# Scores of the latent attention: three rounded products in place of one plain fp32 product

## The reference

```
c      = rmsnorm(c_kv, kv_norm)                         # 512 tokens x 128
q_lat  = einsum('bthd,hdc->bthc', qh, w_uk) * 64**-0.5  # 6 heads, 512 queries x 128
logits = einsum('bqhc,bqkc->bqhk', q_lat, c_sel)        # over the selected tokens
prob   = softmax(where(valid, logits, -inf))
o_lat  = einsum('bqhk,bqkc->bqhc', prob, c_sel)
out    = einsum('bqhc,hcd->bqhd', o_lat, w_uv)
```

## Time and profile before

| | |
|---|---|
| median of three runs | 3670.35 us |
| profiled execution | 3665.43 us |
| its span, first to last instruction | 3663.6 us |
| mean granted TensorE clock | 0.991 of full speed |
| TensorE busy, weight loads | 3566.1 us, 3092.2 us |
| VectorE, ScalarE, GpSimd busy | 2024.6, 1430.8, 176.9 us |
| DMA | 303.22 MB, mean 83 GB/s |

### The profile page before, as it was taken

The page is one execution under the profiler, slowest core; times in us unless marked ns, Lnnn a source line. Parts: engine busy times, 40 slices in busy tenths (PEclk is TensorE's granted clock), DMA queues, the critical chain, the costliest instruction groups (busy, mean ns, idle before and its releaser), DMA issues. The chain is left out here.

```text
span 3663.6 us, 61588 instructions
## 1 busy us (share of the span) xinstructions
PE 3566.1 (97%) x26295; PEld 3092.2 (84%) x26295; DVE 2024.6 (55%) x3372; ACT 1430.8 (39%) x2289; POOL 176.9 (5%) x220
## 2 busy tenths in 40 slices
PE   9999999899999999999999999999999999999998
PEld 8999999788899998888877678888888877678887
DVE  7667663544476646544478564444444468664443
ACT  6844332554453323322244353223232244353222
POOL 0000000111000001000004100000000004100000
PEclk9999999999999999999999999999999999999999
DMA  3232333122223332333320023333333320023332
GB/s 137 81 99 81 93 88 92 65 77 76 68 71 93 91 90 80 98 97 95 115 75 3 24 81 98 98 91 105 95 96 94 111 86 3 24 70 98 98 93 80
DMA packets 87873, 303.22 MB, mean 83 GB/s; under 512 B 9632, under 2 KB 11808, under 8 KB 87344
## 3 DMA queue, kind: packets, MB, share of 16 engines
q1 hardware_dynamic: 87600, 299.28, 26.6%
HBM read 297.11 MB, written 2.13 MB: 82 GB/s over the span
## 5 line engine op out<-in xcount | busy, mean ns | idle before, releaser
L698 DVE TENSOR_TENSOR two_w_lo<-one_raw,two_w_hi 128x1024 fp32r<-128x1024 f32 (+1 forms) x333 | 399.3, 1200 | 749.9 <-ACT two_w_hi L690 747.7
L713 PE MATMUL psum<-two_x_hi,two_w_hi 128*128 128x512 f32 x1768 | 695.1, 393 | 1.1 <-DVE two_rows L1592 0.9
L713 PE MATMUL psum<-two_x_hi,two_w_lo 128*128 128x512 f32 x1768 | 688.4, 389 | 0.0
L713 PE MATMUL psum<-two_x_lo,two_w_hi 128*128 128x512 f32 x1768 | 688.0, 389 | 0.0
L690 ACT CAST two_w_hi<-one_raw 128x1024 fp32r<-128x1024 f32 (+1 forms) x333 | 340.9, 1025 | 803.0 <-PE psum L713 803.0
L713 PEld LDWEIGHTS psum<-two_x_hi,two_w_hi 128*128 128x128 f32 x1768 | 331.8, 188 | 91.3 <-issue 22.1
L2404 PE MATMUL psum<-one_x_hi,one_w_hi 128*128 128x264 f32 (+1 forms) x1376 | 391.6, 285 | 7.9 <-DVE one_x_lo L798 7.3
L713 PEld LDWEIGHTS psum<-two_x_hi,two_w_lo 128*128 128x128 f32 x1768 | 331.9, 188 | 69.7
L713 PEld LDWEIGHTS psum<-two_x_lo,two_w_hi 128*128 128x128 f32 x1768 | 332.0, 188 | 69.5 <-issue 1.4
L2404 PE MATMUL psum<-one_x_lo,one_w_hi 128*128 128x264 f32 (+1 forms) x1376 | 389.3, 283 | 0.0
L2404 PE MATMUL psum<-one_x_hi,one_w_lo 128*128 128x264 f32 (+1 forms) x1376 | 388.7, 282 | 0.0
(11 more groups left out here) (563 smaller groups left out, 6733.9 us busy)
## 6 DMA issues: line engine op xcount, KB each, us to landing
one_raw<-in_swi_in SPq DMA_DIRECT2D x172, 512.0 KB, 3.6
one_raw<-in_ffn_in SPq DMA_DIRECT2D x88, 512.0 KB, 3.8
one_raw<-in_swi_out SPq DMA_DIRECT2D x64, 448.0 KB, 3.3
one_raw<-in_mix_in SPq DMA_DIRECT2D x54, 512.0 KB, 3.6
one_raw<-in_attn_w SPq DMA_DIRECT2D x32, 512.0 KB, 3.9
one_raw<-in_swi_out SPq DMA_DIRECT2D x32, 512.0 KB, 3.6
one_raw<-in_ffn_out SPq DMA_DIRECT2D x32, 448.0 KB, 3.3
one_raw<-in_lru_w SPq DMA_DIRECT2D x24, 512.0 KB, 5.2
```

The lines of the kernel that those rows point to most:

```text
L698: self.nc.vector.tensor_tensor(lo, self.m.raw[:, u % self.RAW, 0:self.cols(u)], hi.bitcast(FP32), ALU.subtract).then_inc(self.s["w_lo"], 1)
L713: last = self.nc.tensor.matmul(self.m.ps[:, bank, :], a[:, w], b[:, k0 + k, :], start=(start and k == 0 and q == 0), stop=(stop and k == n ...
```

## The change

Queries and tokens are split. ScalarE's eviction of a latent query now writes the rounded part (`q_hi`), and VectorE subtracts that from the scaled product in PSUM (`query_rest`, `q_lo`). ScalarE copies the normalised tokens to a rounded tile (`c_hi`), VectorE subtracts again (`c_lo`). Each score is lo x hi, hi x hi and hi x lo in one PSUM group. A bank of the latent queries is now free when VectorE's subtraction is done, so TensorE waits for `q_rest` where it waited for `q_out`. On VectorE, the eviction of score 3 goes behind the subtractions 2 and 3, and L3642 behind all of them.

```diff
+    m.late_q_hi = place("late_q_hi", [P, 6, SEQ], hidden, FP32R)
+    m.late_q_lo = [place("late_q_lo", [P, 5, SEQ], hidden + 60 * KB + 8 * 532 * 4, FP32R),
+                   place("late_q_lo5", [P, 1, SEQ], hidden + 60 * KB + 6 * 532 * 4, FP32R)]
+    m.late_c = Split(place("late_c_hi", [P, SEQ], base + KT * T1 * 4 + (19 * SEQ + 384) * 4, FP32R),
+                     place("late_c_lo", [P, SEQ], hidden + 52 * KB + 2 * SEQ * 4, FP32R))
...
 tensor, latent_query(h):
                     pe.wait_ge(s["q_out"], h - 1)
+                    pe.wait_ge(s["q_rest"], h - 1)
 tensor, score(i):
                     if b == 0:
-                        pe.wait_ge(s["c_ready"], 1)
-                        pe.wait_ge(s["q_out"], h + 1)
-                    nc.tensor.matmul(m.ps[:, bank(i), 0:(b + 1) * QB], e.qlat[:, h, b * QB:(b + 1) * QB],
-                                     c_lat[:, 0:(b + 1) * QB], start=True, stop=True).then_inc(s["scored"], 1)
+                        pe.wait_ge(s["c_rest"], 1)
+                        pe.wait_ge(s["q_rest"], h + 1)
+                    out, queries, n = m.ps[:, bank(i), 0:(b + 1) * QB], slice(b * QB, (b + 1) * QB), (b + 1) * QB
+                    nc.tensor.matmul(out, e.q_lo[h][:, queries], e.c_hi[:, 0:n], start=True, stop=False)
+                    nc.tensor.matmul(out, e.q_hi[h][:, queries], e.c_hi[:, 0:n], start=False, stop=False)
+                    nc.tensor.matmul(out, e.q_hi[h][:, queries], e.c_lo[:, 0:n], start=False, stop=True).then_inc(
+                        s["scored"], 1)
 tensor, ahead of the spreads (L3368):
-            pe.wait_ge(s["q_out"], H)
+            pe.wait_ge(s["q_rest"], H)
 scalar:
-                nc.scalar.mul(e.qlat[:, h, :], m.ps[:, 2 + h % 2, :], SCALE).then_inc(s["q_out"], 1)
+                nc.scalar.mul(e.q_hi[h], m.ps[:, 2 + h % 2, :], SCALE).then_inc(s["q_out"], 1)
...
             for h in range(2, H):
                 latent_query(h)
+            act.wait_ge(s["c_ready"], 1)
+            nc.scalar.copy(e.c_hi, c_lat).then_inc(s["c_rounded"], 1)
 vector:
+            def query_rest(h):
+                dve.wait_ge(s["q_out"], h + 1)
+                nc.vector.scalar_tensor_tensor(e.q_lo[h], m.ps[:, 2 + h % 2, :], SCALE, e.q_hi[h].bitcast(FP32), ALU.mult,
+                                               ALU.subtract).then_inc(s["q_rest"], 1)
...
             evict(2)
+            query_rest(0)
+            query_rest(1)
...
             nc.vector.reciprocal(e.factor, e.factor).then_inc(s["f_factor"], 1)
+            query_rest(2)
+            query_rest(3)
             evict(3)
+            query_rest(4)
+            query_rest(5)
+            dve.wait_ge(s["c_rounded"], 1)
+            nc.vector.tensor_tensor(e.c_lo, c_lat, e.c_hi.bitcast(FP32), ALU.subtract).then_inc(s["c_rest"], 1)
             dve.wait_ge(s["ahead_hi"], 1)
```

More of the change, by code:

```diff
@@ L3297, in __init__ @@
         slot = lambda t, i: t[:, i * SEQ:(i + 1) * SEQ]
-        self.qlat = m.low[:, 0:6 * SEQ].rearrange("p (n t) -> p n t", t=SEQ)
+        self.q_hi = [m.late_q_hi[:, h, :] for h in range(6)]
+        self.q_lo = [*[m.late_q_lo[0][:, h, :] for h in range(5)], m.late_q_lo[1][:, 0, :]]
+        self.c_hi, self.c_lo = m.late_c.hi[:, :], m.late_c.lo[:, :]
         self.olat = m.high[:, 0:6 * SEQ].rearrange("p (n t) -> p n t", t=SEQ)
@@ L3348, in mixers_end_stage @@
                "f_factor", "spread", "normed", "c_squared", "c_gained", "c_sums", "c_root", "c_factor", "c_spread", "c_ready",
-               "c_psum", "tok_ready", "q_psum", "q_out", "scored", "evicted",
+               "c_psum", "tok_ready", "q_psum", "q_out", "q_rest", "c_rounded", "c_rest", "scored", "evicted",
                "shift_ready", "exp_done", "own", "gained", "boosted", "prob_ready", "probT_psum", "probT_ready", "out_psum", "out_ready",
```

## The result

The changed kernel takes 3679.02 us (median of 20 runs, 3670.06 to 3688.63); the kernel before takes 3668.03 beside it (20 runs, 3662.91 to 3674.91). The ratio is 1.0029, with an interval of 1.0021 to 1.0038: about 11 us slower, where the prediction had 0.4 us less and a range that ended at 3678. Times follow the mean granted clock of each run: the two shortest, 3670.06 and 3670.94, had 0.989, the longest, 3688.63, had 0.982. The profiled execution took 3683.35 us at 0.985.

What follows compares the result with a forecast made beforehand. TensorE, 97% busy, was taken as the bound in the last attention steps; other steps wait for VectorE. Head +0.35 and +0.5, loop 2 x -0.6: -0.4 us, so 3665.0 profiled, 3670.0 on the median; range 3662 to 3678.

Steps and rivals of the forecast that it cites:

- the loop's 128-column term: Six 128-column scores per layer: three hidden by waits, three count, one of them twice at half clock; +0.4 us.
- if the clock shares stay: Condition on the two stretches' forecast lengths, about 88.6 and 87.1 us: time at 1.2 GHz unchanged.
- The clock: Rival: one 1.2 GHz stretch more or less in each layer, plus or minus 3.4 us, 3666.6 or 3673.4; chance 0.16.
- The new waits make the head thinner: Clock rival's slower way: TensorE may fall to 1.2 GHz in the head once more, 3673.4; half of chance 0.16.
- denser scores may do the reverse: Clock rival's faster way: one 1.2 GHz stretch less in each layer, 3666.6; half of chance 0.16.
- The rival of dear narrow products: Rounded 128-column products cost 0.222 us, the pace of plain ones, in each layer's first six steps; +4.5, 3674.5; chance 0.11.
- 256 columns: Loop's six 256-column scores per layer: no long wait for probabilities, so all six count; -0.4 us.
- 384 columns: Loop's six 384-column scores per layer: five hidden by waits or ScalarE-set steps, one counts; -0.1 us.
- 512 columns: Loop's six 512-column scores per layer: three hidden by waits or VectorE's work, three count; -0.5 us.
- The head: Stage before the loop: query 4 newly waits for VectorE's subtraction; +0.35 us in the first layer, +0.5 in the second.
- two signs of this: In the head: L3425 0.35 and 0.5 us later; late L3646 following the 1.21 us subtraction without gap means VectorE bounds.
- Theory A of the expectations: From the experiments: at 128 columns weight loads set the pace, operands move half the time; low traffic keeps clock down.

Runs made afterwards that it cites:

- the second experiment: Changed kernel with three rounded products per score (hi x hi three times), but head and waits as before, no remainders or subtractions; 3678.76 us, 1.0025 to the kernel before.
- the first two experiments: From the changed kernel: all scores plain with its head kept, 3671.80 us, 1.0004; three rounded products with the head of before, 3678.76 us, 1.0025.
- the padded and filled kernel: Changed kernel with 128-column scores made 256 wide and five unused 512-column rounded products at the stage's end; 3663.04 us, 0.9988 to the kernel before.

## Why the prediction was wrong

**The step that failed** is the clock in the loop's 128-column term. That one score "falls into a half-clock stretch" carried the stretch of before over unchanged, and the whole sum stood on "if the clock shares stay". Of that term's +0.4 us a layer the narrow steps measured +3.9 and +4.1 (20.96 and 21.07 against 17.05 and 16.99); the 256-column steps of after add 2.8 and 0.8 to that, 13.71 and 11.63 us in place of the 10.87 that they take at full clock in the second experiment.

The clock stood among the rivals, with sign open, and the price of one stretch was about right: the second experiment's narrow steps, at clock 0.90 and 0.75, spend a fifth and a half of their 17.26 and 20.46 us at the lower level, 3.5 and 10.2 us, so 3.2 us go with 6.8, 1.6 for each 3.4, where the rival had 1.7. Its count was wrong, one stretch more in each layer, where the loop has four more and three more. So was its reason. "The new waits make the head thinner" is refuted as the cause of the loss by the first two experiments, and "denser scores may do the reverse" had it backwards for the narrow ones. I took a fuller TensorE for a safer clock, and did not ask what the clock would do under narrow rounded products, of which before has no row.

**What held, at equal clock.** The rounded steps of the second experiment's first layer against those of before:

- 128 columns: +0.2 (17.26 against 17.05), predicted +0.4. The rival of dear narrow products falls: starts are 0.11 us apart.
- 256 columns: 10.87 against 11.18, -0.3, predicted -0.4.
- 384 columns: 13.11 against 13.43, -0.3, predicted -0.1: more of them count than I had taken to stand ahead of a wait.
- 512 columns: 11.03 + 10.66 to the last eviction against 11.33 + 10.75, -0.4, predicted -0.5. The last score-to-score period is 2.02 us (2138.69 to 2140.71 in after), where it was 2.19 and 2.0 was forecast.

Together -0.8 us a layer, where the sum had -0.6. That gain is real, and the clock takes back several times as much. Rounding nothing but the wide scores shows no gain, 1.0004; half a microsecond a layer is below what runs can tell.

**The head.** From the stage's first matmul to the first latent score, with 3.4 us at 1.2 GHz inside, it takes 22.64 us before (second layer) and 22.83 after (first); with 6.8 us inside, 24.27 (first) and 24.66 (second): +0.2 and +0.4, where +0.35 and +0.5 were forecast. The forecast named two signs of this, and the timeline of after shows them:

```profile
2072.87 1.09 ACT L3531 ACTIVATE two_late_q_hi<-psum 128x512 fp32r<-128x512 f32 x2 [2.31 <-PE psum L3386]
...
2076.32 0.86 PE L3436 MATMUL psum<-two_ring,two_misc 128*64 128x384 f32 x2
...
2078.86 1.22 DVE L3668 TENSOR_TENSOR two_ahead_lo<-two_ahead_raw,two_ahead_hi 128x1024 fp32r<-128x1024 f32 x1
2079.99 2.06 DVE L3672 TENSOR_TENSOR two_ring<-two_ring,psum 128x512 f32<-128x512 f32 x3
```

Counted from the eviction of queries 2 and 3, L3436 (L3425 before) starts after 3.45 us, against 2.63 in the earlier trace rows; in the second layer after 3.08 (3194.03 to 3197.11) against 2.43 in the earlier trace rows. That is 0.8 and 0.65 later, where 0.35 and 0.5 were forecast, but the clocks differ: 2.2 of these 3.45 us lie at 1.2 GHz against 0.4 of 2.63, in the second layer 0.6 against none. At 1.6 us for each 3.4 that can make up to 0.8 and 0.3 of the delay. Part of it is given back before the first score. And the three scalings (L3672, L3646 before) follow the 1.22 us subtraction without a gap: VectorE is the head's bound there, as the other sign had it. It costs a few tenths of a microsecond.

**The account.** First stage: 13.7 us more at 1.2 GHz in the loop and 3.4 less in the head, at 1.6 for each 3.4 us, give +4.8; with -0.8 and +0.2 that is +4.2, and +4.3 was measured. Second: 10.3 us more in the loop and 3.4 more in the head give +6.4; with -0.8 and +0.4 that is +6.0, and +5.9 was measured. The head's stretches vary in all kernels alike; what belongs to the change is the loop's 13.7 and 10.3 us, 11 us together. The median lost the same, though its runs need not split it so.

**What stays open:** what it is in the narrow rounded products that the clock answers to. With two, three or four of them a score the clock stays down, with the same three at 256 columns it doesn't; further the runs don't go. Theory A of the expectations got the runs with 256 columns alone, padding, two and four products right and the one with 128 columns alone wrong; the reason that it gives was not tested by itself. Further open are why plain 256-column scores didn't bring the clock back at once, and the stretch behind the stage.

## What to carry to other kernels

Price a change on TensorE at the clock that the stretch will have after it, not at the one it had: read the granted clock of the stretch, and if it already falls there, suspect a change that puts narrow rounded products, each with its weight load, in place of plain ones. Rounded products in place of plain fp32 are shorter at equal clock where they are wide (0.3 to 0.4 us for six scores here, less than these runs can tell); where they are 128 columns narrow, padding them to 256 costs 0.01 us a product and was worth about 11 us here. A gain of tenths per step is lost to a few microseconds at half clock, so clock comes first in the account and instruction counts second.

## What the runs showed of the hardware

**A busy TensorE at half clock.** In the narrow steps TensorE shows 19.22 of 20.96 us busy at mean clock 0.74, and 16.33 of 16.33 at 0.66 in the kernel that rounds 128 columns alone. The Trainium skill ("TensorE: Matmul & The Clock Gate", section "HAM oscillation — how this bites in real kernels") explains the fall to the lower level by TensorE standing idle between bursts of matmuls. The fall here comes behind idle time too (1.05 and 0.99 us in the rows above), but these rows show the lower level going on with hardly any. Its table in "Why this matters for your kernels" names padding M as a remedy for matmuls that are thin in M. Here the moving columns of each product were padded, a neighbouring case and not the same one; 1.0029 became 1.0000.

**The floor of a product that needs its own weights.** Rounded products, from the second of a score on, start 0.11 us apart at 128 columns, 0.12 at 256 and 0.23 at 512. At 1.2 GHz those of 128 columns start 0.22 apart, so this floor doubled as the clock halved.

**The clock's return is not settled by the instructions alone.** The second experiment's kernel came back after 3.4 us in one layer and after 17.1 in the other, and the 20 runs of after spread over 18.6 us, those of before over 12.0. Long spells also occur in code that no run changed: the padded and filled kernel has a mean clock of 0.60 over the 30 us from 964, with 23.9 us at 1.2 GHz in one piece, where after has 0.83 in the same code (from 966). One profiled execution is therefore weak evidence for any single spell; the count over 28 layers and the medians carry the argument.
